# Rings of ten and fourteen places instead of eight and eight for the gathered expert rows, from head 13 of 32 on

## The reference, cut to what matters

```python
def chunk_fn(hc):                              # 128 tokens at a time, four chunks
    q = (hc @ wq).reshape(128, 8, 2, 128)      # 8 heads
    s = jnp.einsum('chsd,hskd->chsk', q, subkeys)
    vals, idx = lax.top_k(s, 16)
    cand = vals[:, :, 0, :, None] + vals[:, :, 1, None, :]
    sc, pos = lax.top_k(cand.reshape(128, 8, 256), 16)
    ex = ...                                   # 16 experts of 16384 for each token and head
    g = softmax(sc)
    act = gelu(einsum('chkd,cd->chk', u[ex], hc))
    return einsum('chk,chkd->cd', g * act, v[ex])
```

## Time and profile before

| what | us |
|---|---|
| median of 3 runs | 2161.32 (2153.51 to 2171.27) |
| span of the profiled execution, first to last instruction | 2140.9 |
| DVE busy | 1291.6 (60%) |
| PE busy | 1739.1 (81%) |
| POOL busy | 1171.9 (55%) |
| ACT busy | 620.4 (29%) |

### The profile page before, as it was taken

One profiled execution on the slowest core, in us unless ns is written; L12 is line 12 of the kernel. 1 busy time (PEld: TensorE's weight loads), 2 busy tenths in 40 slices (PEclk: granted clock), 3 DMA queues, 4 the chain that ended last, 5 costly groups with the idle time before them and its releaser, 6 DMA issues.

```text
span 2140.9 us, 25754 instructions
## 1 busy us (share of the span) xinstructions
PE 1739.1 (81%) x8614; PEld 875.4 (41%) x8614; DVE 1291.6 (60%) x3250; ACT 620.4 (29%) x1497; POOL 1171.9 (55%) x1555
## 2 busy tenths in 40 slices
PE   6998999988888868789879887667767777676776
PEld 3544445777756323344434432223223222232232
DVE  1289863777656956555565655647556565655543
ACT  3256512454542313122222222112212212221111
POOL 2100014556535666666666666666666666666664
PEclk8999999999999998999999998889898889898899
DMA  7466464545399898999999999999999999999997
GB/s 246 130 201 219 161 186 123 149 109 149 64 328 339 295 377 334 362 390 391 379 391 383 383 369 371 378 358 391 358 382 364 364 371 377 372 371 363 378 369 298
DMA packets 282156, 659.70 MB, mean 308 GB/s; under 512 B 71248, under 2 KB 120496, under 8 KB 282032
## 3 DMA queue, kind: packets, MB, share of 16 engines
q0 software_dynamic: 150336, 552.67, 67.7%
q1 hardware_dynamic: 131696, 105.46, 16.5%
HBM read 635.49 MB, written 22.54 MB: 307 GB/s over the span
## 4 chain that ended last, share of the span: by engine, by line
PE 31%; issue 13%; POOL 13%; DMA 7%; another core or an unknown queue 5%; DVE 2%; ACT 2%; ACTq 1%; POOLq 0%; DVEq 0%
PE banks L2113 23%; POOL arena L1662 12%; DMA arena<-in_peer_v_dram,arena 5%; PE banks L2134 4%; PE banks L564 1%; PE banks L1561 1%; DMA arena<-in_peer_u_dram,arena 1%; DVE arena L2063 1%; ACTq L1369 1%; PE banks L2142 0%; ACT arena L1716 0%; PE banks L1142 0%; ACT L1813 0%; ACT L1738 0%
## 5 line engine op out<-in xcount | busy, mean ns | idle before, releaser
L2113 PE MATMUL banks<-arena 128*128 128x512 f32 x1984 | 985.9, 647 | 298.8 <-issue 243.6
L2063 DVE CUSTOM_DVE_ANT_0 arena<-arena,banks 128x1024 f32<-128x1024 f32 x503 | 612.0, 1218 | 386.0 <-DMA arena<-in_peer_u_dram,arena 322.7
L2113 PEld LDWEIGHTS banks<-arena 128*128 128x128 f32 x1984 | 390.9, 205 | 879.2 <-issue 836.5
L1662 POOL DMA_INDIRECT arena<-in_peer_v_dram,arena x504 | 479.2, 951 | 336.3 <-remote 128.4
L1662 POOL DMA_INDIRECT arena<-in_peer_u_dram,arena x512 | 484.3, 946 | 174.1 <-issue 149.8
L1716 ACT ACTIVATE arena<-arena 128x128 f32<-128x128 f32 x496 | 182.0, 397 | 858.6 <-remote 360.5
L1142 PE MATMUL banks<-arena 64*64 64x64 f32 (+1 forms) x2688 | 108.8, 231 | 14.8 <-POOL arena L796 7.0
L2744 PE MATMUL banks<-arena 128*128 128x512 f32 x224 | 110.9, 602 | 0.7 <-ACT arena L2389 0.7
L1142 PEld LDWEIGHTS banks<-arena 64*64 64x64 f32 x2688 | 95.9, 136 | 29.8 <-issue 12.2
L2134 PE MATMUL banks<-arena 128*128 128x384 f32 x256 | 85.8, 486 | 0.0
L2840 PE MATMUL banks<-arena 128*128 128x512 f32 x192 | 84.8, 597 | 0.4 <-issue 0.4
(11 more groups left out here) (365 smaller groups left out, 2001.5 us busy)
## 6 DMA issues: line engine op xcount, KB each, us to landing
arena<-in_w_mod_dram SPq DMA_DIRECT2D x18, 1024.0 KB, 7.4
arena<-in_peer_wq_dram SPq DMA_DIRECT2D x16, 1024.0 KB, 6.7
arena<-in_w_in_dram SPq DMA_DIRECT2D x27, 512.0 KB, 8.0
arena<-in_peer_u_dram,arena POOLq DMA_INDIRECT x512
arena<-in_peer_v_dram,arena POOLq DMA_INDIRECT x512
arena<-in_w_mod_dram SPq DMA_DIRECT2D x3, 2048.0 KB, 11.6
bk_scratch<-arena POOLq DMA_DIRECT2D x8, 768.0 KB, 4.9
kr_scratch<-arena POOLq DMA_DIRECT2D x8, 768.0 KB, 6.7
```

Of the source, the lines that this page charges most:

```text
L1662: pool.indirect_dma_start(ring[:, j % RING, :], None, table, bass.IndirectOffsetOnAxis(ap=idx[:, hi % 4, j:j + 1].bitcast(U32), axis=0)).t ...
L2063: nc.vector.tensor_tensor_reduce(u_ring[:, j % RING, :], u_ring[:, j % RING, :], h2_row, 1.0, 0.0, ALU.mult, ALU.add, acts[:, h % 2, j:j + ...
L2113: m = nc.tensor.matmul(PO[h][:, :], diag[:, j % 4], v_ring[:, j % RING, 512 * h:512 * h + 512], start=hp == 0 and j == 0, stop=hp == HEADS ...
```

## The change

The two tables' rings get more places from head 13 on. The words of `SC0` (2 places) are added to the ring of u, those of `yconv`, `gate` and `bonus` (6 places) to that of v. From head 13 on, gather n of a table (n counted from head 13's first) goes into place n mod 10 (u) or n mod 14 (v), and waits for the dot or product 10 or 14 slots back. The added places wait, the first time, for the last late scores. Up to head 12 places and waits are as before. The order in which POOL issues is unchanged, and so are the 4 diagonal buffers and the count of all instructions that compute or move data.

Each place needs a semaphore, 8 more in all. They are had by letting ten loads of the late stages share semaphores that loads of the first stages had used; their waits count on from the earlier value.

```diff
 RING = 8
+WIDE = 13
+U_RING = 10
+V_RING = 14
...
-    rows_loaded = sem("rows_loaded")
+    rows_loaded, ROWS_BEFORE = wmod_loaded[4], 16
...
-    wout_loaded = [sem(f"wout_half_loaded{i}") for i in range(2)]
+    wout_loaded, WOUT_BEFORE = context_loaded, 16
...
-    wq_loaded = [sem(f"wq_loaded{i}") for i in range(2)]
-    wq_first, wq_low, wq_high = sem("wq_first"), sem("wq_low"), sem("wq_high")
+    wq_loaded, WQ_BEFORE = win_loaded[0:2], 16 * (1 + 2 * PAIRS)
+    wq_first, wq_low, wq_high = wmod_loaded[1:4]
+    WQ_EARLY_BEFORE = 16
...
-    u_rows = [sem(f"u_rows{i}") for i in range(RING)]
-    v_rows = [sem(f"v_rows{i}") for i in range(RING)]
+    u_rows = [sem(f"u_rows{i}") for i in range(U_RING)]
+    v_rows = [sem(f"v_rows{i}") for i in range(V_RING)]
...
-            pe.wait_ge(wout_loaded[0], 16)
+            pe.wait_ge(wout_loaded[0], WOUT_BEFORE + 16)
...
+    halves = [a.rearrange("p a b -> p (a b)")[:, D * i:D * i + D] for a in (SC0, yconv, gate, bonus) for i in range(2)]
+    PLACES = [[u_ring[:, i] for i in range(RING)] + halves[0:2], [v_ring[:, i] for i in range(RING)] + halves[2:8]]
+    ROWS_LANDED = [u_rows, v_rows]
+
+    def place(kind, g, j):
+
+        if g < WIDE:
+            return j % RING, 2 * g + j // RING
+        n = NSL * (g - WIDE) + j
+        r = len(PLACES[kind])
+        return n % r, n // r + (2 * WIDE if n % r < RING else 0)
+
+    def held_before(kind, g, j):
+
+        s, fills = place(kind, g, j)
+        if not fills:
+            return None
+        if g < WIDE:
+            return (g, j - RING) if j >= RING else (g - 1, j + RING)
+        n = NSL * (g - WIDE) + j - len(PLACES[kind])
+        return (WIDE + n // NSL, n % NSL) if n >= 0 else (WIDE - 1, RING + s)
+
+    def row_set(kind, g, j):
+
+        s, fills = place(kind, g, j)
+        return PLACES[kind][s], ROWS_LANDED[kind][s], 16 * fills + 16
...
-            if not (first and hi == 0 and j < RING):
-                pool.wait_ge(used, NSL * g + j + 1 - RING)
-            pool.indirect_dma_start(ring[:, j % RING, :], None, table,
+            held = held_before(kind, g, j)
+            if held is not None:
+                pool.wait_ge(used, NSL * held[0] + held[1] + 1)
+            elif g:
+                pool.wait_ge(late_scores_done, 2 * HEADS)
+            row, landed, _ = row_set(kind, g, j)
+            pool.indirect_dma_start(row, None, table,
                                     bass.IndirectOffsetOnAxis(ap=idx[:, hi % 4, j:j + 1].bitcast(U32), axis=0)
-                                    ).then_inc(sems[j % RING], 16)
+                                    ).then_inc(landed, 16)
...
-                    dve.wait_ge(u_rows[j % RING], 32 * g + 16 * (j // RING) + 16)
-                    nc.vector.tensor_tensor_reduce(u_ring[:, j % RING, :], u_ring[:, j % RING, :], h2_row, 1.0, 0.0, ALU.mult, ALU.add,
+                    row, landed, n = row_set(0, g, j)
+                    dve.wait_ge(landed, n)
+                    nc.vector.tensor_tensor_reduce(row, row, h2_row, 1.0, 0.0, ALU.mult, ALU.add,
                                                    acts[:, h % 2, j:j + 1]).then_inc(dots, 1)
...
-                pe.wait_ge(v_rows[j % RING], 32 * g + 16 * (j // RING) + 16)
+                row, landed, filled = row_set(1, g, j)
+                pe.wait_ge(landed, filled)
                 for h in range(2):
-                    m = nc.tensor.matmul(PO[h][:, :], diag[:, j % 4], v_ring[:, j % RING, 512 * h:512 * h + 512],
+                    m = nc.tensor.matmul(PO[h][:, :], diag[:, j % 4], row[:, 512 * h:512 * h + 512],
                                          start=hp == 0 and j == 0, stop=hp == HEADS - 1 and j == NSL - 1)
```

More of the change, by code:

```diff
@@ L318, in _layer @@
     latents_loaded = [sem(f"latents_loaded{i}") for i in range(NT)]
-    context_loaded = [sem(f"context_loaded{i}") for i in range(NTC)]
-    wmod_loaded = [sem(f"wmod_loaded{i}") for i in range(len(MOD_SLABS))]
+    context_loaded = [sem(f"context_then_wout_loaded{i}") for i in range(NTC)]
+    wmod_loaded = [sem(f"wmod_then_others_loaded{i}") for i in range(len(MOD_SLABS))]
     constants_made = sem("constants_made")
@@ L335, in _layer @@
     hT_context = sem("hT_context_columns")
-    win_loaded = [sem(f"win_loaded{i}") for i in range(3)]
+    win_loaded = [sem(f"win_then_wq_loaded{i}") for i in range(3)]
     projections_made = sem("projections_made")
@@ L1234, in tail @@
             apply_chunk(NBLK - 1, 1)
-            pe.wait_ge(wout_loaded[1], 16)
+            pe.wait_ge(wout_loaded[1], WOUT_BEFORE + 16)
             pe.wait_ge(y_gated, 6)
@@ L1321, in put @@
             pool.wait_ge(rows_finished, n[0])
-        pool.wait_ge(rows_loaded, 16 * 2)
+        pool.wait_ge(rows_loaded, ROWS_BEFORE + 16 * 2)
         pool.wait_ge(rows_finished, 2)
@@ L1340, in pool5 @@
             nc.gpsimd.tensor_tensor(total, total if k else first, part, ALU.add).then_inc(y_summed, 1)
-        pool.wait_ge(rows_loaded, 16 * 4)
+        pool.wait_ge(rows_loaded, ROWS_BEFORE + 16 * 4)
         pool.wait_ge(head_norm_vector, head_step(4, 6))
@@ L1551, in queries @@
             if h == 0:
-                pe.wait_ge(wq_first, 16)
+                pe.wait_ge(wq_first, WQ_EARLY_BEFORE + 16)
             elif h == 1:
-                pe.wait_ge(wq_low, 48)
+                pe.wait_ge(wq_low, WQ_EARLY_BEFORE + 48)
             elif h == 4:
-                pe.wait_ge(wq_high, 64)
+                pe.wait_ge(wq_high, WQ_EARLY_BEFORE + 64)
             for a in range(2):
@@ L1628, in last_row @@
         if j < RING:
-            return v_ring[:, j], v_rows[j], 32 * LAST_HEAD + 16
-        return u_ring[:, j - RING], u_rows[j - RING], 32 * LAST_HEAD + 48
+            return row_set(1, LAST_HEAD, j)
+        row, landed, n = row_set(0, LAST_HEAD, j)
+        return row, landed, n + 16
     out_v = out[0].rearrange("(t p) d -> t p d", p=P)
@@ L1657, in gather @@
         def gather(kind, g, hi, j, first):
-            ring, table, sems, used = [(u_ring, peer_u[0], u_rows, dots), (v_ring, peer_v[0], v_rows, experts_added)][kind]
-            if not (first and hi == 0 and j < RING):
-                pool.wait_ge(used, NSL * g + j + 1 - RING)
-            pool.indirect_dma_start(ring[:, j % RING, :], None, table,
+            table, used = [(peer_u[0], dots), (peer_v[0], experts_added)][kind]
+            held = held_before(kind, g, j)
[5 more added lines that the diff above has]
+            pool.indirect_dma_start(row, None, table,
                                     bass.IndirectOffsetOnAxis(ap=idx[:, hi % 4, j:j + 1].bitcast(U32), axis=0)
-                                    ).then_inc(sems[j % RING], 16)
+                                    ).then_inc(landed, 16)
         def body(t, first):
@@ L2125, in late_query @@
         def late_query(i):
-            pe.wait_ge(wq_loaded[i // 2 % 2], 16 * (i // 4) + 16)
+            pe.wait_ge(wq_loaded[i // 2 % 2], WQ_BEFORE + 16 * (i // 4) + 16)
             if i == 0:
```

## The result

Over 20 runs of each kernel the changed one takes 2171.53 us (median; 2155.87 to 2181.16), the one before 2160.06 us (2144.34 to 2171.27). The ratio is 1.0057, with a 95% interval from 1.0034 to 1.0080. The change loses 0.6%, some 12 us, where I had forecast a gain of 0.3%. The profiled execution of after has a span of 2163.8 us, that of before 2140.9 us. These two single executions lie further apart than the medians, so their rows tell places and kinds, and the ratio tells the size.

A forecast was written before the change was run, and what follows sets the result against it. The gathers' DMA was taken as the bound, with v gathers stalled by late reports of finished products. The cycle balance (-5.1) and first filling (-1.4) gave -6.5 us, other terms 0: 2161.3 to 2155 us; overall range 2098 to 2178.

The forecast's parts named there:

- my 25.5 stalls: POOL, 1240 to 2100 us: 106 us above the gap before v gathers, at 4.16 us a stall, one in 33.7 us.
- The sign of PE's longer stretches: PE after a stall: products run at 1.80 us for longer, with rows waiting, if the forecast is right.
- u gathers unchanged: POOL's u gathers: sign of a right forecast, idle time stays at the bare gap of 0.305 us each.
- All stalls go: Rival, v gathers: deeper ring outlasts late reports and stalls from 1296 on vanish, 75 us gained, 2086 us; chance 0.14.
- rarer stalls: Rival, v gathers: 6 slots lengthen the cycle to 49 us, 23 us gained, 2138 us; chance 0.22.
- more places for u: 0: Ring of u, 8 to 10 places: nothing waits there, so alone worth 0; 5.1 us of patience for late dots.
- my slower rival: DVE's late top-k steps make u gathers stall too, 3.1 us every second cycle, 40 us lost, 2201 us; chance 0.10.
- The cycle balance: v ring, 8 to 14: 0.7 more reports lengthen the cycle from 33.7 to 36.0 us at 3.1 us loss; gain 5.1 us.
- The end: between -3 and +5; I take 0: Kernel's end: PE makes up 6 more rows, 10.8 us, before the last row lands 30 us later; taken as 0.
- the bold sentence: Expert stage: word that a product is done reaches ACT and POOL late while DMA engines run at 409 GB/s.
- No rate to win: Rival, gathers: 371 GB/s is the memory's average, 409 only follows a rest; smoother flow gains nothing, 2161 us; chance 0.08.
- the 80 us of "loss": 1240 to 2100 us: running at 371 instead of 409 GB/s loses 80 us, the most a ring can win.

The follow-up runs named there:

- v freed: Kernel before, but products of heads 14 to 29 read constant words and v gathers wait only for the landing 8 back: ratio 1.0143.
- without its wait: Changed kernel, but from head 14 on ACT makes diagonals 8 to 11 behind the exponentials and the gelu: ratio 1.0074 to the kernel before.
- the run with the narrow end: Changed kernel, but v gathers of heads 29 to 31 wait for the product 8 slots back again: ratio 1.0035 to the kernel before.
- the run with four memsets: Kernel before with four 128x2 memsets behind every gather of both tables from head 14 on: 2157.1 us in a single run, beside 2146.5 of before.
- the half-row run: Kernel before, but v gathers from head 13 on fetch 2 KB rows instead of 4 KB: 2145.7 us in a single run, beside 2147.3 of before.

## Why the prediction was wrong

**What held.** Of the signs that I had named for my forecast these came: v idle above the gap 96 us (95 to 105 named), and a first stall that comes later (behind the group at 1294 and 1300 us the next is at 1351, where before it was 1325 behind 1296). The count of 23 to 25 stalls holds only if neighbouring waits are taken as one, about 25 groups. I had got my 25.5 stalls by dividing by one stall of 4.16 us, and didn't count them; there were 38 waits of over 1 us in 27 groups. The sign of PE's longer stretches tells little. The change has such stretches (21.20 us for 44 records, above), but the kernel before had them as well, beside the 10.83 us of the earlier trace rows:

```profile
1448.70 22.55 PE L2113 MATMUL banks<-arena 128*128 128x512 f32 x48 [8.41 <-issue]
```

What didn't come was "u gathers unchanged". The core of the balance held: more places fill and the stalls stay. "All stalls go" (2086) and "rarer stalls" (2138) are out. The Trainium skill's rule behind the first ("Trainium Kernel Development and Optimization", Best Practices: consistent bubbles can mean that SBUF ran out) is not borne out here: with 14 places for 8 (96 us of 106), or with v freed (110 us, now before u gathers), the bubbles stay.

**The step that failed first: "more places for u: 0", with u "unchanged".** I let DVE catch up after each stall. It doesn't always: u lost 14 us above the gap in the change, 67 us with 8 places. This was my slower rival, down to its sign (u gathers that idle above 0.31 us). Its price, a loss of 3.1 us in every second cycle, 40 us, was too high for the change and its chance of 0.10 too low: the change's median lost 12 us in all. The 14 us are POOL's idle time; how much of them reached the kernel's time isn't shown.

**The cycle balance, -5.1 us.** All of it was the 0.7 reports more that PE should earn with rows in store, in cycles that get longer "at the same loss of 3.1 us". The cycles did get longer, by the groups 860/27 = 31.9 us before and 860/25 = 34.4 after. The loss of each didn't stay the same, 4.4 us of POOL's time instead of 3.9, and the gain never came: 366 GB/s instead of 371 are 860 x 5/371 = 11.6 us lost, where -5.1 stood. I had kept in the sum only what PE could do with a longer stretch, and left out what hangs on PE's lag. The diagonals wait for products, and behind them on ACT stand the gelu and the exponentials, and on those DVE's weights and dots. That this lag carries the loss is shown in part. With 8 diagonal buffers the loss is gone (0.9988), a u ring of 8 makes it dear (1.0161), and a free v hands the stalls to u (1.0143). But the link by the gelu is refuted as the loss (1.0074 without its wait), and which of the others carries it isn't shown.

**"The end: between -3 and +5; I take 0".** It was 10.5 us in the profiled pair, and 0.2% (some 5 us) by the run with the narrow end. I had let PE work off its 10.8 us of backlog in the 30 us before the last row lands. But PE couldn't: at the last dot it had 6 products more before it than the kernel before (91 records for 67), and in those 30 us its diagonals were still coming late (8.07, 5.23 us [idle before them]). The last head's late weights weren't the reason, since the end was as long (52.3 us) when they came in time.

**The cause under the bold sentence.** "The word that a product is done reaches ACT and POOL late while the DMA engines run at 409 GB/s" named a coincidence. At 285 GB/s the reports were as late. They are late while POOL issues gathers back to back, and at a stall come 4 to 5 us after its last issue (4.47, 4.05 and 4.7 us in three runs). A deeper ring lengthens just this: DVE's late steps of the top-k came to 127.3 us for 51.5.

**"No rate to win" (2161)** was nearest in number, and is not excluded. Against it 402 GB/s were held for 34 us on end in the run with v freed. For it stands the run with four memsets, which has timely reports and 366 GB/s. And the 80 us of "loss" were read too boldly: in the 12 slow us of the earlier trace rows the DMA engines were busy for 0.89, in the fast part for 1.02. By idle engines alone the rate would fall from 409 to 409 x 0.89/1.02 = 357 GB/s, and it was 308, so idleness is half of the dip. The Trainium skill ("HBM Reference", Specifications (TRN2)) gives about 358 GB/s per core in effect. The means of all runs with full rows (333 to 371) lie around that figure, yet in the half-row run the time stays the same at 285. A rate above 371 exists for tens of us; that it can be held as a mean no run shows.

**What stays open.** Why reports are late while POOL issues isn't shown. The half rows exclude the bytes, though not the count of rows. The pause in POOL's issue isn't settled: four small memsets took the v stalls away, one memset of a longer pause took away a third. Nor is it shown why 8 diagonal buffers help the kernel before by 0.4%; its v stalls are as they were (199.3 us), while TensorE's clock is 0.97 for 0.88. And what holds POOL once the reports are timely is open.

## What to carry to other kernels

A ring that stalls its producer isn't thereby too short: ask first whether the consumer is late or only the word that it is done. Here more places gained nothing against a late word. Before a ring is made deeper, follow what queues behind the consumer's other waits (here the diagonals), for its lag may grow by as many slots as the ring does, and at the end of the kernel it has to be worked off. And measure the ceiling first: free the wait altogether, as in the run with v freed, before building the deeper ring. A stall that vanishes without a gain, as with the four memsets, means that something else limits as closely.

## What the runs showed of the hardware

- While POOL issues indirect DMAs of 128 rows one behind the other (0.94 us and a gap of 0.30), waits of ACT, POOL and DVE end late, DVE's for its own steps by 5.5 us too, and the last of them end 4 to 5 us after POOL has stopped. It is the same with rows of 2 KB (4.05 us of idle time) as of 4 KB (4.47 us). With four memsets of 128x2 behind each gather (interval 1.31 us for 1.24) these waits are nearly gone (ACT's 26.7 us for 269.4), and with one memset of 128x128 (1.32 us) they are not (232.2 us).
- POOL got 591 to 607 gathers through in 860 us in every form in which v gathers waited for products: with stalls of 4 us, with more and shorter ones, with pauses, and almost without stalls (598 behind four memsets).
- Three semaphore increments behind a gather didn't lengthen the interval of 1.24 us, and yet changed the rhythm of the stalls. A memset of 128x2 (118 ns) fits into the gap as well; one of 128x128 takes 222 ns.
